# A two-layer mixer and SwiGLU encoder on one core: high and low part of the tokens in one FFN instruction, its epilogue in steps, and a new order at both ends

## What is computed

```python
for i in range(DEPTH):                          # DEPTH = 2
    h = rms_norm(x, mix_norm_g[i])
    proj = h @ w_in[i]                          # columns for all three branches and their gates
    ...                                         # differential attention, two-way state space scan
    y_xa = mem_cross_attention(xa_q, rms_norm(mem, mem_norm_g[i]), w_mem_kv[i])
    merged = g0 * (y_da @ wb_da) + g1 * (y_ssm @ wb_ssm) + g2 * (y_xa @ wb_xa)
    x = x + merged @ w_out[i]
    h = rms_norm(x, ffn_norm_g[i])
    gate, up = split_cols(h @ w_ffn_in[i], (2816, 2816))
    x = x + (silu(gate) * up) @ w_ffn_out[i]
return rms_norm(x, final_norm_g)
```

## Time and profile before

| what | value |
|---|---|
| median of 3 runs | 1423.81 us (1423.7 to 1423.96) |
| the profiled execution's own time | 1424.59 us |
| its span in the profile | 1422.9 us |
| PE busy | 1402.7 us, 99% of the span |
| DVE, ACT, POOL busy | 936.0, 876.6, 337.8 us |
| PE's share of the chain that ended last | 91% |
| DMA | 255.48 MB, mean 180 GB/s |
| TensorE clock granted, mean | 0.998 of full speed |

### The profile page before, as it was taken

How to read it: one execution, slowest core, us unless ns; L and a number is a source line. 1 busy time by engine, 2 the same in 40 slices (tenths; PEclk the granted TensorE clock), 3 DMA queues, 4 the chain that set the end, 5 groups by cost and what they waited for, 6 DMA issues and landing times.

```text
span 1422.9 us, 25302 instructions
## 1 busy us (share of the span) xinstructions
PE 1402.7 (99%) x8877; PEld 1256.5 (88%) x8877; DVE 936.0 (66%) x1223; ACT 876.6 (62%) x1408; POOL 337.8 (24%) x161
## 2 busy tenths in 40 slices
PE   7999999999999999999999999999999999999997
PEld 7899898888888889998899998988888888999986
DVE  5568575898997456554444774768889865555543
ACT  6576677986756454445466666788767464544453
POOL 0410000010023434444323000001010344354442
PEclk9999999999999999999999999999999999999999
DMA  7655445557665555656556554555676555466664
GB/s 244 190 174 176 123 130 176 151 196 220 197 182 191 184 164 168 186 178 237 183 179 181 162 159 129 154 172 159 190 218 218 163 185 185 149 184 186 195 219 148
DMA packets 158497, 255.48 MB, mean 180 GB/s; under 512 B 12730, under 2 KB 58924, under 8 KB 158380
## 3 DMA queue, kind: packets, MB, share of 16 engines
q1 hardware_dynamic: 157819, 252.84, 58.0%
q10 hardware_dynamic: 560, 1.18, 0.2%
HBM read 252.80 MB, written 1.18 MB: 178 GB/s over the span
## 4 chain that ended last, share of the span: by engine, by line
PE 91%; ACT 3%; DVE 2%; DVEq 1%; issue 1%; ACTq 1%; DMA 0%; SPq 0%
PE PS L609 81%; PE S L609 7%; PE S L616 1%; DVE wL L1313 1%; ACT wH L922 1%; ACT scr L1072 1%; PE S L821 0%; PE S L886 0%; PE S L792 0%; DMA regA<-in_mem_dram 0%; DVEq L1486 0%; DVE actLf L1522 0%; ACT actLf L947 0%; PE S L761 0%; DVEq L1524 0%
## 5 line engine op out<-in xcount | busy, mean ns | idle before, releaser
L922 ACT CAST wH<-w_raw 128x1024 fp32r<-128x1024 f32 x443 | 457.9, 1042 | 408.6 <-PE PS L609 356.2
L1313 DVE TENSOR_TENSOR wL<-w_raw,wH 128x1024 fp32r<-128x1024 f32 (+1 forms) x331 | 456.4, 1384 | 347.9 <-ACT wH L922 326.6
L1241 POOL TENSOR_TENSOR wL<-w_raw,wH 128x1024 fp32r<-128x1024 f32 (+1 forms) x112 | 285.6, 2551 | 409.7 <-ACT wH L922 409.7
L609 PE MATMUL PS<-hH,wH 128*128 128x256 f32 (+1 forms) x1488 | 371.0, 287 | 0.0
L609 PE MATMUL PS<-hL,wH 128*128 128x256 f32 (+1 forms) x1488 | 365.3, 283 | 0.0
L609 PEld LDWEIGHTS PS<-hH,wH 128*128 128x128 f32 (+1 forms) x1488 | 284.2, 191 | 3.2 <-issue 2.6
L609 PEld LDWEIGHTS PS<-hL,wH 128*128 128x128 f32 (+1 forms) x1488 | 284.7, 191 | 0.6
L609 PE MATMUL PS<-wH,actH 128*128 128x512 f32 x560 | 224.0, 400 | 0.0
L609 PE MATMUL PS<-wH,actL 128*128 128x512 f32 x560 | 218.7, 391 | 0.0
L609 PE MATMUL PS<-hH,wL 128*128 128x256 f32 (+1 forms) x1488 | 211.0, 283 | 0.0
L609 PEld LDWEIGHTS PS<-hH,wL 128*128 128x128 f32 (+1 forms) x1488 | 192.1, 191 | 0.0
(11 more groups left out here) (237 smaller groups left out, 1512.1 us busy)
## 6 DMA issues: line engine op xcount, KB each, us to landing
w_raw<-in_w_in_dram SPq DMA_DIRECT2D x192, 512.0 KB
w_raw<-in_w_ffn_in_dram SPq DMA_DIRECT2D x176, 256.0 KB
w_raw<-in_w_branch_dram SPq DMA_DIRECT2D x64, 512.0 KB
w_raw<-in_w_ffn_out_dram SPq DMA_DIRECT2D x44, 512.0 KB
w_raw<-in_w_mem_kv_dram SPq DMA_DIRECT2D x35, 512.0 KB
regA<-cs_rows SPq DMA_DIRECT2D x64, 256.0 KB, 4.8
w_raw<-in_w_out_dram SPq DMA_DIRECT2D x16, 512.0 KB
regA<-in_mem_dram SPq DMA_DIRECT2D x6, 512.0 KB, 4.6
```

Source lines behind the costliest of these rows:

```text
L609: return nc.tensor.matmul(o, l, r, start=first, stop=last, skip_group_check=True)
L922: nc.scalar.copy(wH[:, slot].rearrange("p k c -> p (k c)")[:, q], raw[:, slot].rearrange("p k c -> p (k c)")[:, q]).then_inc(h_done[slot], 1)
L1241: nc.gpsimd.tensor_tensor(wL[:, slot].rearrange("p k c -> p (k c)")[:, q], raw[:, slot].rearrange("p k c -> p (k c)")[:, q], wH[:, slot].r ...
L1313: v.tensor_tensor(wL[:, slot].rearrange("p k c -> p (k c)")[:, q], raw[:, slot].rearrange("p k c -> p (k c)")[:, q], wH[:, slot].rearrange ...
```

## The change

**FFN units.** hH and hL become one tile hHL in which, for each of the eight row blocks, the 256 high tokens stand beside the 256 low ones. Groups 1 to 10 get a new layout "C": with a high weight tile stationary, one instruction streams high and low tokens, 512 columns, into a whole bank, the high product in the left half and the low one (the correction) in the right. A group so needs four banks: its PSUM pair and two of the S banks (pair 0 takes S[0], S[1]; pair 1 takes S[2], S[3]). The low weights go on with 256 columns. Group 0 keeps layout T.

**Epilogue.** `hidden` is replaced by steps over four units after a group's end. The added first one copies both corrections out of PSUM on ACT (`hid_corr`), since the two halves must be added; DVE adds, scales the gate and frees the banks (`hid_sum`), ACT takes silu one unit later, DVE multiplies two units later, ACT and DVE split three units later. The up half is no longer scaled there: each token's reciprocal root is applied when the down sums are added to x, in two DVE instructions of 512 columns in place of one add of 1024.

**Loops.** The hardware loops over layers and over FFN groups are gone on every engine; all is written out. Units past the last layer's end are neither loaded nor split, and the memory's steps are left out in the last layer.

**Start.** The memory is turned unnormalized; its reciprocal roots are applied later: to mk's columns through a row that PE broadcasts (`mem_row`, two matmuls per layer, at unit 3), to mv's rows by ACT's scale. SP loads columns 0 to 255 of `mem`, unit 0, the rest of `mem`, units 1 and 2, then the rows; ACT starts the parameter loads. The memory's gains are loaded and turned by themselves; the other parameters are turned at unit 1. ACT squares the memory after the first splits, and starts x's load after that. mk is emptied by DVE.

**End.** The last unit does the first 128 tokens wholly, then the others; DVE, ACT and the store of the first half run beside the second.

The diff, cut:

```diff
-    g += [("ffn", b, 4, "T") for b in range(FT // 2)]
+    g += [("ffn", b, 4, "T" if b == 0 else "C") for b in range(FT // 2)]
...
+    put(1, "pe", "par_turn")
+    put(2, "dve", "params")
+    put(3, "pe", "mem_row")
+    put(4, "dve", "mem_row")
...
+    for b in range(N_FFN):
+        u = first("ffn", b) + 4
+        if b:
+            put(u, "act", "hid_corr", b)
+        put(u, "dve", "hid_sum", b)
+        put(u + 1, "act", "hid_silu", b)
+        put(u + 2, "dve", "hid_mult", b)
+        put(u + 3, "act", "hid_high", b)
+        put(u + 3, "dve", "hid_low", b)
...
+            load_mem(0)
...
+            load(0, 0)
+            load_mem(1)
+            for u in range(1, 3):
                 load(0, u)
...
             def mem_turn(n, b):
                 take(0 if n is None else n, b)
-                pe.wait_ge(mem_scaled, 1 if n is None else n + 2)
+                if b < 2:
+                    pe.wait_ge(mem_in[b], 16 if n is None else 16 * (n + 2))
...
+                if kind == "ffn" and b in (1, 2) and c == 0:
+                    for bank in (2 * pair, 2 * pair + 1):
+                        take(lay, bank)
...
+                elif layout == "C":
+                    banks = [dst[:, 0:512], dst[:, 512:1024], S[2 * pair], S[2 * pair + 1]]
+                    for m in range(4):
+                        for kk in range(UT):
+                            mm(v3(banks[m], 2), wH[:, slot, kk, P * m:P * (m + 1)], hHL[:, UT * c + kk, :, :],
+                               first_unit and kk == 0, False)
+                    pe.wait_ge(l_done[slot], use(lay, u) + 2)
+                    for m in range(4):
+                        for kk in range(UT):
+                            ins = mm(banks[m][:, 0:T], wL[:, slot, kk, P * m:P * (m + 1)], hH[:, UT * c + kk, :], False,
+                                     last_unit and kk == UT - 1)
+                elif kind == "down" and b == 1 and last_unit and lay == DEPTH - 1:
+                    pe.wait_ge(l_done[slot], use(lay, u) + 2)
+                    for t in range(NT):
...
+                        if t == 0:
+                            ins.then_inc(down_half, 1)
...
                 elif kind == "mem_turn":
-                    mem_turn(lay, i)
+                    if lay < DEPTH - 1:
+                        mem_turn(lay, i)
+                elif kind == "mem_row":
+                    take(lay, 0)
+                    pe.wait_ge(mem_diag, lay + 1)
+                    for t in range(NT):
+                        ins = mm(S[0][:, P * t:P * (t + 1)], ones, mdiag[:, t, :], True, True)
+                    ins.then_inc(mem_bcast, 1)
...
+                elif kind == "hid_corr":
+                    g = GI["ffn", i]
+                    pair = g % 2
+                    wait_full(act, lay, g)
+                    nc.scalar.copy(v3(gate_corr, 2), halves(PS[pair][:, :])[:, :, 1, :])
+                    nc.scalar.copy(v3(up_corr, 2), halves(SS[:, 1024 * pair:1024 * (pair + 1)])[:, :, 1, :]
+                                   ).then_inc(corr_out, 1)
...
-            mem_stats(None)
+            act.wait_ge(ident_ready, 1)
+            act.wait_ge(gain_ready, 1)
             for b in range(4):
...
+                mem_high(None, b, gmem[:, 0:8])
+                if b < 3:
+                    split_h(0, b)
+            for t in range(NT):
+                mem_square(None, t)
+            mem_root()
             act.dma_start(xN, x.rearrange("b (t p) d -> p (b t) d", p=P)).then_inc(x_in, 16)
             act.wait_ge(row_in, 16 * ROW_LOADS)
...
+                        dve.wait_ge(corr_out, (N_FFN - 1) * lay + i)
+                        v.tensor_tensor(v3(gate, 2), halves(PS[pair][:, :])[:, :, 0, :], v3(gate_corr, 2), ALU.add)
+                        dve.drain()
+                        v.tensor_tensor(v3(gate, 2), v3(gate, 2), r2, ALU.mult)
+                        dve.drain().then_inc(gate_scaled, 1)
+                        v.tensor_tensor(v3(hid, 2), halves(SS[:, 1024 * pair:1024 * (pair + 1)])[:, :, 0, :],
+                                        v3(up_corr, 2), ALU.add).then_inc(psum_free[pair], 1)
...
+                elif kind == "down" and b == 1 and lay == DEPTH - 1:
+                    for t in range(NT):
+                        if t == 0:
+                            dve.wait_ge(down_half, 1)
+                        else:
+                            wait_full(dve, lay, g)
+                        v.scalar_tensor_tensor(xN[:, t, cols], src[:, UC * t:UC * (t + 1)], xr[:, t:t + 1], xN[:, t, cols],
+                                               ALU.mult, ALU.add)
+                        dve.drain().then_inc(fin_x, 1)
+                        v.tensor_tensor(fin[:, t, cols], xN[:, t, cols], gB[:, cols], ALU.mult)
...
             for t in range(NT):
+                dve.wait_ge(fin_std, t + 1)
+                v.reciprocal(xr[:, t:t + 1], xsum[:, t:t + 1])
+                dve.drain().then_inc(fin_rstd, 1)
+                done = slice(0, D) if t == 0 else slice(UC, D)
+                v.tensor_scalar(fin[:, t, done], fin[:, t, done], xr[:, t:t + 1], None, ALU.mult).then_inc(fin_second, 1)
```

448 lines of the change are left out of this document (233 added, 215 removed).

## The result

The changed kernel takes 1413.93 us (median of six runs, 1412.99 to 1414.94), the kernel before beside it 1423.88 (1423.7 to 1424.12): ratio 0.993, 95% interval 0.992 to 0.994. So it is faster, by 0.7%, as forecast, but by 9.9 us instead of 14.1, and the time lies 0.9 us above the upper end of the range. The profiled execution took 1414.03 us, its span is 1412.3.

What follows compares the result with a forecast made beforehand. PE's own instruction stream was taken as the bound. FFN 8.5, other PE edits 0.8, start 2.2 and tail 2.6 made 14.1 us off 1424.59: 1410.5 for the profiled execution, 1409.7 as median, range 1407.0 to 1413.0.

Steps and rivals of the forecast that it cites:

- What bounds it: Whole kernel: between start and tail only what PE itself issues counts; work on other engines is hidden while on time.
- FFN, 8.5 us: FFN groups 1 to 10: merging pairs of 256-column instructions into 512-column ones saves 0.106 us in each of 80 units.
- 8 x 0.227 + 8 x 0.120: Price of one merged FFN unit, eight wide and eight narrow instructions: 2.774 us, against 2.880 before.
- rival (2): FFN merge: each exchange saves only the skill rule's 2.5 ns, 1.6 us instead of 8.5, so 1416.6; chance 0.07.
- Other edits on PE: PE's stream: dropping four last-layer memory turns saves 1.8 us, two added `mem_row` cost 0.9; net minus 0.8 us.
- The epilogue, 0: FFN group ends: banks come free about 4.9 us after a group's end, wanted at 11.1, so no cost.
- Rival (4): FFN epilogue: PE waits for `psum_free` at 18 places if the chain passes 11.1 us; slower, about 1535; chance 0.03.
- The start, 2.2: Start up to unit 3: memory turned without root or scaling, unit 3 at 20.7 us instead of 22.88; minus 2.2 us.
- at about 7.5: Start: the memory's second part lands at about 7.5 us, with unit 0's 512 KB ahead costing 1.3 at up to 400 GB/s.
- The second limit, ACT at unit 3: Start: ACT's split of unit 3 ends at 20 us, only 0.7 ahead of PE's need.
- Rival (1): Start: it gives nothing because ACT, in order behind the rows, still opens unit 3; 1411.9; chance 0.17.
- The tail, 2.6: After PE's last matmul: 6.7 us to the span's end instead of 9.2; minus 2.6 us.

Runs made afterwards that it cites:

- low_512: Changed kernel with the low weights also streaming 512 columns, adding the product of the two low parts: 1481.59 us.
- start_turned: start_all with the odd units of the merged layout running their low part before their high part: 1411.42 us.
- epi_one: Changed kernel with all steps of a merged group's epilogue behind one unit instead of four: 1413.96 us.
- par_on_sp: Changed kernel with the six parameter loads on SP behind unit 2 instead of on ACT's queue: 1413.39 us.
- mem_first: Changed kernel with the second memory part issued ahead of unit 0 in SP's order: 1412.91 us.
- rows_later: Changed kernel with the sixteen pairs of cs_rows loads one unit later in SP's order: 1413.61 us.
- turned_rows: start_turned plus the later cs_rows loads, x loaded where the changed kernel loads it: 1410.76 us.
- fewer_taps: Changed kernel without the last two of five convolution taps for the sixth channel group, leaving out part of the computation: 1413.79 us.
- unit_99_half: Changed kernel with weight unit 99 only half loaded in both layers (256 KB instead of 512 KB), leaving out part of the computation: 1413.48 us.
- alternate: Changed kernel with 512-column and 256-column instructions by turns in a merged unit, instead of eight and eight: 1414.39 us.
- pool_two: Changed kernel with POOL instead of DVE making the low parts of units 97 and 105: 1417.86 us.
- start_all: Changed kernel with the memory ahead of unit 0, parameter loads on SP behind unit 2, and the square-root table loaded early: 1412.02 us.
- together: start_turned plus later cs_rows loads and the load of x issued behind unit 1's cast: 1414.56 us.

## Why the prediction was right or wrong

**What bounds it: right.** PE is full in all of the FFN, and each microsecond taken from its stream there came off the total.

**FFN, 8.5 us: right mechanism, too large.** It gave 7.05. The paces of the two kinds of instruction were as taken from the earlier trace rows (low_512: 0.2267). The step that failed is "8 x 0.227 + 8 x 0.120": it added prices from stretches of one width. Each change from eight narrow to eight wide costs about 0.019 us (2.793 - 2.774; 0.018 by start_turned), 80 times 1.5 us. low_512 and start_turned show this; what in the engine causes it stays open. The trace of before had it: its first down unit after the FFN takes 1.84 us for eight wide instructions instead of 1.813. And the range, though it let start, tail and row vary, held this term at 8.5: its 1.45 alone is more than the 0.93 by which the time lies outside.

**The rule of the Trainium skill**, "TensorE: Matmul & The Clock Gate", section "Back-to-back issue gap", as the prediction used it, would have had the merge at 1.6 us; measured are 7.0, so rival (2) falls. But the section gives that formula for an isolated instruction; for a stream of weight loads and matmuls, as here, it gives about 131 ns for 512 columns. Here they take 227 (low_512), so the trace disagrees with both figures, and the measurement decides.

**Other edits on PE: right.** The turns gave 1.97 (1.8), the rows cost 0.44 each (0.46).

**The epilogue, 0: right,** and with more room than was shown: even in one place it costs nothing (epi_one). Rival (4) was no danger. But DVE's load did not rise by a fifth, it fell, from 59% to 54% of the time: its splits of weights take 1.23 us in this window where they took 2.01 before.

**The start, 2.2: wrong.** It gave 0.9. The step that failed is the landing "at about 7.5", which took 400 GB/s from one microsecond for the whole transfer. The rate in the microseconds from 4 to 6 is 222 and 310 GB/s in the changed kernel:

```profile
4.00:5.00 1.00, 1.00 (x4) 0.69 (x4) 0.80 (x3) 0.00 (x0) 0.00 (x0) 1.00 0.94 222
5.00:6.00 1.00, 0.09 (x1) 0.00 (x0) 0.43 (x2) 0.37 (x1) 0.00 (x0) 1.00 0.95 310
```

The engines are 94% busy at 222 GB/s. The part landed 1.4 us later than said. The small parameter loads explain little of it: with them issued behind unit 2 the rate is nearly as low and the part came only 0.43 earlier (par_on_sp, first line below). With both parts of the memory ahead of unit 0, and all parameter loads in their old place, the same microsecond moves 391 GB/s (mem_first, second line):

```profile
4.00:5.00 1.00, 0.91 (x4) 0.51 (x3) 0.80 (x3) 0.00 (x0) 0.00 (x0) 1.00 0.92 250
4.00:5.00 1.00, 0.43 (x2) 0.46 (x3) 0.80 (x3) 0.00 (x0) 0.00 (x0) 1.00 1.04 391
```

So it is in every profile of the changed kernel and its variants: 191 to 250 GB/s from 4 to 5 us in the twelve with unit 0 between the two parts, 376 to 415 in the five with unit 0 behind them. The low rate comes with that order; why is open. Unit 0's 512 KB so cost 2.0 us (mem_first), where 1.3 had been priced. And even without it the second part landed at 6.9 us (issued at 1.30, 5.6 later), not at the 5.84 that the forecast started from. That more of unit 0 would run at the slow pace was right (four more instructions, three taken). The second limit, ACT at unit 3, was named rightly and took over as soon as the first was gone. Rival (1) was half right in its time (0.9 us, between its 0 and the 2.2) and wrong in its reason: in the changed kernel PE did not wait for ACT at unit 3.

**The tail, 2.6: 0.5 too much.** The chain went as laid out: DVE began 1.32 before PE's end (1.36), and the last store left 1408.76 - 1405.21 = 3.55 behind it (3.45). But from there it took 3.54 us to the end of the span, from ACT's queue, where 3.23 had been taken from a store of SP. That is 0.3 of the 0.5; 0.1 is the passes and 0.1 rounding.

**What was missing altogether: 0.6 us at unit 109.** The step that failed is "between the start and the tail only what PE itself has to issue counts": it was read from PE's waits over the whole run, and does not hold in a stretch where DVE is 90% busy. There a part of a single late landing reaches PE. The reason is in SP's order, which the change did not touch: SP's wait for PE's diag step. The landing of the same unit took 6.2 us before and 7.7 after, though both kernels issue it in the same place; why just 1.5 us more is open. It is those 1.5 us that matter: in layer 1 SP waits as long for PE (7.7 us), but there ACT waits 2.89 us for the load, DVE not at all, and nothing is lost. That the order of SP is what lets it be late is shown by rows_later and turned_rows, and DVE's part by fewer_taps and unit_99_half.

In sum: 1.45 (FFN) + 1.3 (start) + 0.6 (unit 109) + 0.5 (tail) = 3.85, less 0.2 won at the turns and rows, against 1414.03 - 1410.5 = 3.5 missed in the profiled execution; 0.1 is rounding.

## What to carry to other kernels

Price a mixture of instructions from a row where the mixture stands, and look at the change from one kind to the next before adding up prices of pure stretches. For the first microseconds take no DMA rate from the best microsecond of another order of loads: here the order alone moved it from 391 to 222 GB/s. Give every term of the sum a width in the range, the one that seems safest too. And where a side engine is 90% busy, look in the queue of the engine that issues its loads for a wait on something else: a load queued behind it is late for a reason that no busy share shows.

## What the runs showed of the hardware

- Eight instructions of 512 columns behind eight of 256 take 1.84 us instead of 1.813; a unit of both loses 0.019. In steady alternation a pair loses 0.007 (alternate, one execution), and among their like they lose nothing (low_512).
- With POOL's two-input pass beside it, a DVE pass of 0.69 us takes 1.33 to 2.54 us (pool_two).
- ACT loads a table (1.28 us) in front of its first scaled copy when none is loaded: at 5.63 in the changed kernel. An early root takes it off the path: in start_all the load stands at 1.79, while ACT waits.
- A PE that stood idle for 3.66 us came back at a granted clock of 0.50 and 0.21 us per 256 columns, for 5.25 us of work (together).
- From 4 to 5 us the DMA engines moved 222 GB/s at 94% busy with unit 0's load between the memory's two parts, and 391 with it behind them (after, mem_first).
- Small loads take far longer than their size: 32 KB of a broadcast row landed 7.0 us after its issue (turned_rows), and 10.6 with a megabyte from another queue beside it (together).
